# Layer norms with the shift added by ScalarE, and the last norm with tokens on the partitions

## The reference, cut to what matters

```
def layer_norm(x, g, b):
    mu = jnp.mean(xf, axis=-1, keepdims=True)
    var = jnp.mean(jnp.square(xf - mu), axis=-1, keepdims=True)
    return ((xf - mu) * lax.rsqrt(var + LN_EPS) * g + b).astype(x.dtype)

x <- layer_norm(alpha * x + sublayer(x), g, b)
```

## Time and profile before

| | |
|---|---|
| median of 3 runs | 1884.14 us (1883.71 to 1886.66) |
| the profiled execution's own time | 1878.84 us |
| its span, first to last instruction | 1876.8 us |
| mean granted TensorE clock | 0.936 |
| PE busy | 1674.6 us, 89% |
| DVE busy | 633.0 us, 34% |
| ACT busy | 549.1 us, 29% |
| POOL busy | 722.6 us, 39% |

### The profile page before, as it was taken

How to read it: one execution, slowest core, us unless ns; L and a number is a source line. 1 busy time by engine, 2 the same in 40 slices (tenths; PEclk the granted TensorE clock), 3 DMA queues, 4 the chain that set the end, 5 groups by cost and what they waited for, 6 DMA issues and landing times. The chain is left out here.

```text
span 1876.8 us, 37967 instructions
## 1 busy us (share of the span) xinstructions
PE 1674.6 (89%) x15074; PEld 1520.0 (81%) x15074; DVE 633.0 (34%) x1282; ACT 549.1 (29%) x1064; POOL 722.6 (39%) x510
## 2 busy tenths in 40 slices
PE   4699798869878869899999998998889899999996
PEld 4599677646656649899999997987659899999996
DVE  1211110434454546611111128326465711111127
ACT  1222000135544433432222213216432432222311
POOL 3453232323335436554434325503026564434320
PEclk8899799679999989899999998998979999999998
DMA  6633887035535524143223223222404143223201
GB/s 224 197 89 110 244 261 243 12 115 181 158 114 157 160 73 142 53 133 97 85 85 102 81 67 90 82 67 68 146 12 138 54 135 91 87 84 105 85 15 46
DMA packets 297172, 210.54 MB, mean 112 GB/s; under 512 B 34286, under 2 KB 290467, under 8 KB 296483
## 3 DMA queue, kind: packets, MB, share of 16 engines
q1 hardware_dynamic: 278490, 166.27, 30.2%
q10 hardware_dynamic: 10696, 21.78, 3.6%
q0 software_dynamic: 7808, 20.05, 3.5%
HBM read 197.97 MB, written 18.42 MB: 115 GB/s over the span
## 5 line engine op out<-in xcount | busy, mean ns | idle before, releaser
L1593 PE MATMUL ps<-x_high,w_high_t 128*128 128x256 f32 (+1 forms) x1488 | 427.3, 287 | 12.5 <-POOL w_low_t L1516 7.6
L1516 POOL TENSOR_TENSOR w_low_t<-w_raw,w_high_t 128x1024 fp32r<-128x1024 f32 (+1 forms) x130 | 307.7, 2376 | 326.8 <-ACT w_high_t L1621 326.8
L1594 PE MATMUL ps<-x_low,w_high_t 128*128 128x256 f32 (+1 forms) x1488 | 423.4, 285 | 0.0
L1595 PE MATMUL ps<-x_high,w_low_t 128*128 128x256 f32 (+1 forms) x1488 | 422.7, 284 | 0.0
L1593 PEld LDWEIGHTS ps<-x_high,w_high_t 128*128 128x128 f32 x1488 | 283.8, 191 | 16.2 <-POOL x_low L1526 7.9
L1594 PEld LDWEIGHTS ps<-x_low,w_high_t 128*128 128x128 f32 x1488 | 283.6, 191 | 0.3
L1595 PEld LDWEIGHTS ps<-x_high,w_low_t 128*128 128x128 f32 x1488 | 282.9, 190 | 0.0
L1621 ACT CAST w_high_t<-w_raw 128x1024 fp32r<-128x1024 f32 (+1 forms) x130 | 132.1, 1025 | 147.8 <-PE ps L1595 123.5
L1705 DVE TENSOR_TENSOR h_t<-silu_t,ps 128x256 f32<-128x256 f32 (+1 forms) x88 | 37.4, 425 | 359.4 <-PE ps L1595 354.9
L1593 PE MATMUL ps<-hid_high,w_high_t 128*128 128x264 f32 (+1 forms) x542 | 154.4, 285 | 0.0
L1594 PE MATMUL ps<-hid_low,w_high_t 128*128 128x264 f32 (+1 forms) x542 | 153.6, 283 | 0.0
(11 more groups left out here) (338 smaller groups left out, 3263.6 us busy)
## 6 DMA issues: line engine op xcount, KB each, us to landing
w_raw<-in_ffn_w_gu SPq DMA_DIRECT2D x88, 512.0 KB, 3.8
pages<-in_cache_slc SPq DMA_DIRECT2D x192, 128.0 KB
rows<-in_cache_cmp SPq DMA_DIRECT2D x123, 128.0 KB, 4.0
w_raw<-in_ffn_w_down SPq DMA_DIRECT2D x32, 448.0 KB, 3.7
w_raw<-in_gla_w_in SPq DMA_DIRECT2D x24, 512.0 KB, 3.6
rows<-in_cache_cmp ACTq DMA_DIRECT2D x70, 128.0 KB, 5.1
pages<-in_cache_slc POOLq DMA_DIRECT2D x64, 128.0 KB, 2.8
w_raw<-in_ffn_w_down SPq DMA_DIRECT2D x16, 512.0 KB, 4.0
```

Source lines behind the costliest of these rows:

```text
L1516: nc.gpsimd.tensor_tensor(low(u)[:, 0:k], raw[:, u % RAW, 0:k], high(u)[:, 0:k].bitcast(F32), ALU.subtract).then_inc(low_done, 1)
L1593: nc.tensor.matmul(psum(i), high(u)[:, k, :], a[0][:, at, c], start=(k == 0), stop=False)
L1594: nc.tensor.matmul(psum(i), high(u)[:, k, :], a[1][:, at, c], start=False, stop=False)
L1595: ins = nc.tensor.matmul(psum(i), low(u)[:, k, :], a[0][:, at, c], start=False, stop=(k == t.kc - 1))
```

## The change

Four things are edited, all in `phase_trunk` (t0 and t1).

1. **Shift on ACT.** In the six half norms that have a next stage DVE keeps only the multiplication, and counts it on a new semaphore `scaled`; ACT adds the shift (`shift_of`, an activation with a bias, in place in `xT`) and then makes the copy, one tile behind.
2. **Another form of the adds.** The running sum and the three folds are `scalar_tensor_tensor` with a multiplication by 1.0, with the same two operands in SBUF as before.
3. **The last norm by token.** Both halves of the last norm leave the old path. Their un-normed columns are transposed, so that tokens lie on the partitions; ACT copies the blocks out of PSUM and sums them in the same instruction (`turned`), DVE makes the mean, ACT squares with the mean as bias and an accumulated sum and takes the root of one column (`deviation`), and DVE does the rest with gain and shift as rows (`normed_by_token`). Blocks 0 and 1 are turned ahead of passes e+3 and e+5, e being the last pass of the first half (`first_half`), and go through ACT and DVE at passes e+3 to e+7. Blocks 2 to 4 follow the last pass. No running sum is made for this norm.
4. **Tables.** Gain and shift are loaded for it, each spread over 128 partitions (512 KB each), by SP at the start of t1, ahead of the weights of unit 4.

```diff
@@ phase_trunk, on SyncE @@
+            if store is not None:
+                for dst, table in ((store.gain, "ln_g"), (store.shift, "ln_b")):
+                    sp.dma_start(dst[:], io[table][1, 1:2, :].to_broadcast([P, D_MODEL])).then_inc(y_tabs, 16)
             for u, t in enumerate(units):
...
-                    sp.wait_ge(tr_act, t + 1)
-                    sp.wait_ge(tr_dve, t + 1)
+                    sp.wait_ge(y_done, t + 1)
@@ on TensorE @@
+            def turn(t):
+                if t == 0:
+                    pe.wait_ge(centred, 2 * NNORM)
+                    pe.wait_ge(std_done, NNORM)
+                    pe.wait_ge(out_done, walk.others[first_half + 1])
+                elif t == 2:
+                    pe.wait_ge(out_done, walk.others[NPASS])
+                if 1 <= t <= 2:
+                    pe.wait_ge(y_sum, 2 * t)
+                for f in range(2):
+                    for k in range(4):
+                        ins = nc.tensor.transpose(ps[0:ROWS[t], y_bank(t, f), k * P:(k + 1) * P],
+                                                  xT[:, 4 * f + k, t * P:t * P + ROWS[t]], cst["ident"][:])
+                    ins.then_inc(tr_done, 1)
...
+                if store is not None and i in (first_half + 3, first_half + 5):
+                    turn((i - first_half - 3) // 2)
...
             if store is not None:
-                pe.wait_ge(normed, KT * NNORM)
                 for t in range(2, len(ROWS)):
-                    for hf in range(2):
-                        turn(t, hf)
+                    turn(t)
@@ on ScalarE @@
+            def shift_of(n, k):
+                x = xT[:, k, cols(norms[n][1])]
+                act.wait_ge(scaled, n * KT + k + 1)
+                nc.scalar.activation(x, x, ACT.Identity, bias=shift(n)[:, k:k + 1]).then_inc(normed, 1)
+
             def turned(t):
+                r = slice(0, ROWS[t])
+                if t == 2:
+                    act.wait_ge(mm_done, NPASS)
+                for f in range(2):
+                    act.wait_ge(tr_done, 2 * t + f + 1)
+                    nc.scalar.activation(store.y[t][r, f * 512:(f + 1) * 512], ps[r, y_bank(t, f), :], ACT.Copy,
+                                         accum_out=store.sums[r, t, f:f + 1]).then_inc(y_sum, 1)
+
+            def deviation(t):
+                r = slice(0, ROWS[t])
+                act.wait_ge(y_mean, t + 1)
+                act.wait_ge(folded, 3 * NNORM)
+                nc.scalar.activation(sq[r].rearrange("p k n -> p (k n)")[:, 0:D_MODEL], store.y[t][r, :], ACT.Square,
+                                     bias=store.mean[r, t:t + 1], accum_out=store.var[r, t:t + 1]).then_inc(y_sq, 1)
+                act.wait_ge(y_sq, t + 1)
+                nc.scalar.activation(store.std[r, t:t + 1], store.var[r, t:t + 1], ACT.Sqrt, bias=cst["eps"][r],
+                                     scale=1.0 / D_MODEL).then_inc(y_std, 1)
...
-                    for k in range(KT):
-                        act.wait_ge(normed, n * KT + k + 1)
-                        nc.scalar.copy(X[0][:, k, c], xT[:, k, c]).then_inc(xh_done, 1)
+                    for k in range(KT + 1):
+                        if k < KT:
+                            shift_of(n, k)
+                        if k:
+                            act.wait_ge(normed, n * KT + k)
+                            nc.scalar.copy(X[0][:, k - 1, c], xT[:, k - 1, c]).then_inc(xh_done, 1)
...
+                turned(2)
+                turned(3)
+                deviation(2)
+                turned(4)
+                deviation(3)
+                deviation(4)
@@ on VectorE @@
+            def normed_by_token(t):
...
+                dve.wait_ge(y_std, t + 1)
+                nc.vector.reciprocal(store.std[r, t:t + 1], store.std[r, t:t + 1]).then_inc(y_rstd, 1)
...
+                nc.vector.scalar_tensor_tensor(out=y, in0=y, scalar=store.mean[r, t:t + 1], in1=store.gain[r, :],
+                                               op0=ALU.add, op1=ALU.mult).then_inc(y_part, 1)
...
+                nc.vector.scalar_tensor_tensor(out=y, in0=y, scalar=store.std[r, t:t + 1], in1=store.shift[r, :],
+                                               op0=ALU.mult, op1=ALU.add).then_inc(y_done, 1)
...
-                        nc.vector.tensor_tensor(total[:, hf, 0:w], xT[:, 0, c] if t.m == 1 else total[:, hf, 0:w], x,
-                                                ALU.add).then_inc(sum_done, 1)
+                        nc.vector.scalar_tensor_tensor(out=total[:, hf, 0:w],
+                                                       in0=xT[:, 0, c] if t.m == 1 else total[:, hf, 0:w], scalar=1.0,
+                                                       in1=x, op0=ALU.mult, op1=ALU.add).then_inc(sum_done, 1)
...
-                        nc.vector.tensor_tensor(sq[:, 0:half, 0:w], sq[:, 0:half, 0:w], sq[:, half:2 * half, 0:w],
-                                                ALU.add).then_inc(folded, 1)
+                        nc.vector.scalar_tensor_tensor(out=sq[:, 0:half, 0:w], in0=sq[:, 0:half, 0:w], scalar=1.0,
+                                                       in1=sq[:, half:2 * half, 0:w], op0=ALU.mult, op1=ALU.add)\
+                            .then_inc(folded, 1)
...
-                    for k in range(KT + 1):
-                        if k < KT:
-                            x = xT[:, k, c]
-                            ins = nc.vector.scalar_tensor_tensor(out=x, in0=x, scalar=gain(n)[:, k:k + 1],
-                                                                 in1=sd[:, 0:w], op0=ALU.mult, op1=ALU.mult)
...
-                            nc.vector.tensor_scalar(x, x, shift(n)[:, k - 1:k], None, ALU.add).then_inc(normed, 1)
+                    for k in range(KT):
+                        x = xT[:, k, c]
+                        nc.vector.scalar_tensor_tensor(out=x, in0=x, scalar=gain(n)[:, k:k + 1], in1=sd[:, 0:w],
+                                                       op0=ALU.mult, op1=ALU.mult).then_inc(scaled, 1)
```

More of the change, by code:

```diff
@@ L1334 @@
 Unit = namedtuple("Unit", "W col k0 kc src what m first last dst")
+Final = namedtuple("Final", "y gain shift sums mean var std")
 SPLIT = ((0, 256), (256, NTOK))
@@ L1416, in phase_trunk @@
     NU, NPASS, NNORM = len(units), walk.n, len(norms)
+    if store is not None:
+        NNORM -= 2
+        before_last, first_half = norms[NNORM - 1][2], norms[NNORM][2]
+        norms = norms[:NNORM]
     TURN = -NU % RING if then is not None else 0
@@ L1436, in phase_trunk @@
         dve_own = sem("dve_own")
-        sum_done, mean_done, centred, squared, folded, var_done, std_done, normed, xh_done, xl_done = (
+        sum_done, mean_done, centred, squared, folded, var_done, std_done, scaled, normed, xh_done, xl_done = (
             sem(n) for n in ("ln_sum", "ln_mean", "ln_centred", "ln_squared", "ln_folded", "ln_var", "ln_std",
-                             "ln_normed", "x_high", "x_low"))
-        tr_done, tr_act, tr_dve, y_out = sem("ytr"), sem("ytr_act"), sem("ytr_dve"), sem("y_out")
+                             "ln_scaled", "ln_normed", "x_high", "x_low"))
+        tr_done, y_sum, y_mean, y_sq, y_std, y_rstd, y_part, y_done, y_tabs, y_out = (
+            sem(n) for n in ("ytr", "y_sum", "y_mean", "y_sq", "y_std", "y_rstd", "y_part", "y_done", "y_tabs", "y_out"))
         block = ctx.enter_context(nc.Block())
@@ L1470, in cols, with norm_at, y_bank @@
             return slice(*SPLIT[hf])
+        def norm_at(i, after):
+            return [n for n in walk.norm_at(i, after) if n < NNORM]
+        def y_bank(t, f):
+            return (6, 6, 6, 0, 2)[t] + f
         def psum(i):
@@ L1519, in _ @@
             for i in range(-1, NPASS):
-                for n in walk.norm_at(i, 5):
-                    if store is not None and n >= NNORM - 2:
-                        continue
+                for n in norm_at(i, 5):
                     c = cols(norms[n][1])
@@ L1599, in _ @@
                     mean_of(n)
-                if e + 2 >= NPASS and store is not None:
-                    pe.wait_ge(normed, KT * n)
-                    pe.wait_ge(out_done, walk.others[NPASS])
-                    for t in range(2):
-                        for hf in range(2):
-                            turn(t, hf)
                 if e + 5 >= NPASS:
@@ L1645, in _ @@
                     hidden_high(i)
-                for n in walk.norm_at(i, 1):
+                for n in norm_at(i, 1):
                     w, c = width(norms[n][1]), cols(norms[n][1])
@@ L1653, in _ @@
                             .then_inc(squared, 1)
-                    if store is not None and n == NNORM - 1:
-                        turned(0)
-                        turned(1)
                 for u in walk.cast_at(i):
@@ L1659, in _ @@
                         round_high(u)
-                for n in walk.norm_at(i, 4):
+                if store is not None and first_half + 3 <= i <= first_half + 6:
```

(18 more changed lines are left out.)

54 lines of the change are left out of this document (23 added, 31 removed).

## The result

The changed kernel takes **1856.97 us** (median of 4 runs, 1854.96 to 1857.82) where the kernel before, on the same chip, took 1883.99 (4 runs, 1883.71 to 1886.66): a ratio of 0.9852, with a 95% interval from 0.9835 to 0.9869. That is 27.0 us less, where 20 were forecast, and 1 us inside the 1856 to 1872 of the forecast's own case. Its profiled execution took 1857.82 us, its span is 1855.8 us and the mean granted clock 0.938, against 1878.84, 1876.8 and 0.936.

What follows compares the result with a forecast made beforehand. PE, busy 89% of the span, bounds the kernel; time is to be had where it waits or runs slowly, in three norms and the end. 12 + 8 = 20 us off 1884.14 gives 1864.1 us, range 1853 to 1877.

Steps and rivals of the forecast that it cites:

- the forecast's own case: Norms and program end both gain, 12 to 28 us together, giving 1856 to 1872 us; chance 0.66.
- Rival (a): In the three norms, adds in the new form don't wait for POOL's low parts: 43 us gained, 1841 us; chance 0.13.
- (b): The three norms give 0 to 3 us, only the end counts: 8 to 11 us gained, some 1875 us; chance 0.14.
- (c): At the start of t1 table loads make unit 4's weights 39 us late: slower, 1903 us; chance 0.04.
- Part 1: Shift moved to ACT in the three norms with a next stage: 12 us gained, bounds 3 and 23 us.
- Part 2: New form of running sums and folds: no gain; first-half fold waits of 5.8 us stay.
- Part 3: Last norm by token at the program's end: 8 us gained, between 6.5 and 9.5, DVE setting the end.
- Part 4: Gain and shift tables loaded ahead of unit 4's weights at the start of t1: 3 us of loading, no cost.
- the cover of 5.9: At the start of t1, unit 4's weight load can come 5.9 us later before PE would wait.
- The sum: 12 us from the norms and 8 from the last norm, 20 us off the median of 1884.14: 1864.1 us.

Runs made afterwards that it cites:

- the two kernels on the form of the adds: Changed kernel with the shift back on DVE (last norm and new adds stay): 1874.0 us; changed kernel with plain tensor_tensor adds: 1858.51 us.

## Why the prediction was right, and where its sizes were off

**What bounds the kernel, and rivals.** Held. PE's waits in the norms and the tail behind the last product were the places, and no other stretch gave anything. The shift's move and the last norm each give their part alone: 19.8 and 9.3 us timed, 29.1 added up, where both in one kernel gave 27.1 beside them; 16.4 and 4.7 in the traces, 21.1 added up, where both gave 24.0. They add up only to within 2 to 3 us. Rival (a) fell with the two kernels on the form of the adds, (b) with the shift alone, (c) with the tables' landing.

**Part 1: 12 us forecast, 16.6 found in the trace** (counted from the first norm of each trunk to its last product, with what the transposes cost in t1 taken out). The mechanism was the one written down: sums off the path, mean matmul earlier, a new wait on the folds of the second half. The term that was mis-sized is the 1.0 us for one `x_low` and one DVE instruction. Eight `x_low` took 7.07 us, 0.88 apiece, not 8.0, and the low parts behind them 9.67, not 9.90. The mean of the second half therefore comes 6.1 us earlier relative to the first, not 5.4, and the folds end 12.0 us behind the last `x_low`, not 12.5. Up to the second variance matmul the three norms gained 6.1, 6.5 and 5.6 us, 18.2 together where I had 14.2. What follows it I put at 2.2 us of loss (4.2 for clock, less 2 for `x_low`) and it was 1.6. The new waits were to be 2.9 each and were 2.35, 0.48 and 2.36. I had taken the 0.96 us of one multiplication beside an `x_low` for the step of the sequence, rounded up. That is the length of one instruction, and instructions that follow each other overlap: the earlier trace rows has two multiplications in 0.88 us, though one alone shows 0.48 in the trace of after, and the 0.96 overlaps its neighbours by the same 0.08. The step was 0.88 all along. Nor do four of each eight multiplications take such a time, as part 2 of the prediction has it: it is three, 18 of the 48, which changes nothing in the argument. I also took 0.62 us a tile for ACT; it was 0.71, since an activation with a bias takes 0.51 where a copy takes 0.39. It cost nothing: `x_low` steps at 0.88.

**Part 2: nothing, and it was nothing.** The first halves' folds wait for 1.65, 2.43 and 1.64 us, 5.7 together, against 5.8 in the earlier trace rows.

**Part 3: 8 us forecast, 7.5 found.** The tail is 8.9 us shorter (25.1 to 16.2), as forecast with 16 us behind the last product. Block 2 was ready for DVE 5.9 us behind the last product (I had 6.1), DVE took 8.1 us for three blocks (7.8), and 2.2 follow. PE's stream grew by 1.4 us from the first mean matmul to the last product of t1, measured against the kernel with the shift alone, where I had 0.8: the sixteen transposes set its products back by 1.7 us, the mean and variance matmuls that left it had cost 0.8; the rest of 0.5 I did not trace. It was DVE that set the end, as forecast.

**Part 4: nothing, and it was nothing.** The cast of unit 4 came 4.0 us later into t1, where I had taken 3, and the cover of 5.9 held it. The stretch of t1 ahead of its first norm does take 0.7 us more than before (27.7 in place of 27.1), but it takes 0.6 more in the kernel with the shift alone, which loads no tables; what it is stays open.

**The sum.** 16.6 + 7.5 = 24.1 us by parts. The stretches ahead of the first norms of t0 and t1 take 0.8 us more (0.1 and 0.7) and the one between the trunks, the same code in both, 0.45 less, which leaves the 23.8 from the start of t0 to the end. The medians differ by 27.0. The last step, "I take the same 20 us from" the median, went by one execution of before that was 5.2 us below its median, and the second profiled one was 4.2 below that of its group, while the profiled one of after was 0.9 above its own. So some 3 us of the measured gain lie where no two traces show them. Of the 7 us by which the gain exceeds the forecast, about 4 are the sizes of part 1, and these 3 are the rest. The code ahead of t0 is the same, and it varies by 5.6 us over ten traces; whether the changed kernel gains there on average, or the profiled executions of before were lucky ones, these runs don't settle.

## What to carry to other kernels

Look for the instruction that stands in a list ahead of something another engine waits for, and move it to an engine with time to spare, even at a higher price there: a shift takes 0.35 us on DVE when nothing holds it up (0.53 on average as it stood) and 0.51 on ACT, and moving eight of them in each half took 16 us off the path. Then ask for what is late next: the new wait here was 2.4 us twice and was had back by asking one pass later, in one line. And where a step repeats, size it by the engine that sets its pace over the whole sequence (eight `x_low`), and by the distance from start to start, not by the length of one instruction.

## What the runs showed of the hardware

The shift on DVE was itself one of those that stood behind POOL, though it reads one operand in SBUF only. I had overlooked it. The second half of the first norm of t1 in the kernel before, DVE and then POOL:

```profile
1487.74 0.35 DVE L1759 TENSOR_SCALAR xT<-xT,vec 128x264 f32<-128x264 f32 x1
1488.01 0.99 DVE L1752 SCALAR_TENSOR_TENSOR xT<-xT,vec,ln_sd_t 128x264 f32<-128x264 f32 x1
1488.92 0.84 DVE L1759 TENSOR_SCALAR xT<-xT,vec 128x264 f32<-128x264 f32 x1
1489.68 0.48 DVE L1752 SCALAR_TENSOR_TENSOR xT<-xT,vec,ln_sd_t 128x264 f32<-128x264 f32 x1
```

```profile
1487.94 1.66 POOL L1526 TENSOR_TENSOR x_low<-xT,x_high 128x264 fp32r<-128x264 f32 x2 [13.35 <-ACT x_high L1671]
```

A shift takes 0.35 us, and 0.84 beside an `x_low`. The Trainium skill, "SBUF — State Buffer", section "Who interferes with whom", names `tensor_scalar` among the VectorE instructions that can contend with GpSimd where their operands meet certain conditions. The 0.84 us agrees. On ACT all 48 shifts take 0.49 to 0.52 us, those beside an `x_low` too, so the move took away both the instruction and its collisions. No run here separates the two.

How much a collision costs depends on the partner's length. A sum of 0.43 us takes 0.52 among the `x_low`, 0.88 apart, and 2.16 among low parts of 2.5. In a chain of three folds the turn was lost every time: 6.54 us for work of 2.40. An `x_low` takes 0.74 us alone, and 0.88 from start to start beside DVE.
